# The attention stage of a two-stack float32 network on one core: dense tiles moved between attention units, and the stage's evictions rewritten

## Chip, core and metric

One core of a Trainium2 chip runs the whole program. The metric is the device time of one execution in microseconds (us).

## What is computed

256 tokens of width 1024, float32, pass through a first stack of four layers (each: half a SwiGLU block, a mixer, half a SwiGLU block) and a second stack of two layers. The change touches only the mixer of the second stack, so it is executed twice, once in each of its layers. Cut to that part, the reference is:

```
h = h + 0.5 * swiglu(rms_norm(h, g0), wi, wo)
n = rms_norm(h, g1)
aq, ak, av, bq, bkc, bvc, bks, bvs, bkw, bvw, bgate, cq, ck, cv, ga, gb, gc = split(n @ w_in)
ya = diff_attention(aq, ak, av)
yb = nsa_attention(bq, compress(bkc), compress(bvc), bks, bvs, bkw, bvw, sigmoid(bgate))
yc = swa_sink_attention(cq, ck, cv)
merged = sigmoid(ga)*(ya @ wb[0]) + sigmoid(gb)*(yb @ wb[1]) + sigmoid(gc)*(yc @ wb[2])
h = h + merged @ w_out
h = h + 0.5 * swiglu(rms_norm(h, g2), wi2, wo2)
```

Branch A has 4 heads with two score maps each and a norm of each head's output, branch B 8 heads with three kinds of keys each, branch C 8 heads.

## The kernel before

**Weights.** Every weight tile is 1 MB (128 x 2048 floats). SyncE loads it into one of RING = 3 `raw` buffers. ScalarE rounds it to `w_hi` (L513, in `split_hi`), VectorE subtracts to get `w_lo` (L891, in `split_lo`), and TensorE forms each product of three matmuls, hi*hi, lo*hi and hi*lo (L1584 to L1586, in `matmul3`). Tile n+3 may overwrite `w_hi`/`w_lo` of tile n only when TensorE has counted up `tile_used` for n. The helper that both engines call for this is `consumed(n)`, here ScalarE's (L515; VectorE's, L894, calls `split_lo`):

```
def consumed(n):
    act.wait_ge(tile_used, seen.next(tile_used))
    split_hi(n + RING)
```

Each engine runs its own instruction list in order, and the lists are written out by hand.

**PSUM.** Eight banks of 128 x 512 floats: `acc0..3` (attention scores and transposed probabilities, and the accumulators of the output projection) and `up0..3` (projections, attention outputs, gates).

**The stage (`mix`: ScalarE L740, VectorE L1362, TensorE L1940, GpSimd L2294)** has five parts.

1. A norm. `turn_norm` (L1646) keeps TensorE busy with dummy matmuls (L1644) until VectorE has 1/rms as a diagonal, and then transposes and scales x by matmuls against it (L1653). The norms before feed-forward blocks are of another kind (`norm_xs`): x is transposed unscaled by `turn_x` (L1665, matmuls at L1669), the first half of it inside the block before, and 1/rms is multiplied in when results leave PSUM. The tuple `XS` (L36) says which stages get that kind.
2. Projections: 19 weight tiles one after another. Nine are of 2 x 8 x 3 matmuls with 256 tokens moving (`up_matmuls`), three hold a key half of that kind and a value half of 128-column matmuls (`key_value`, L1951), four are the compression's hidden layer (`hidden`, L1962), two are for `AV` with 512 columns moving, and one has 24 columns (the gates of branch B).
3. Attention: 40 units (8 of A, 24 of B in the order sel, win, cmp, 8 of C) in steps i = 0 to 45. In step i TensorE forms the scores of unit i (L1742, L1743, or L2153 for cmp), transposes unit i-3 (L1749 to L1751, L2160) and multiplies values of unit i-4 (L2031 to L2033, L2055, L2056, L2052). VectorE reduces the scores (L1133), ScalarE takes exp (L657) and copies the transposed unit (L665), GpSimd scales (L2241).
4. Merge: per branch and half of the width, two gate tiles and one branch tile, 18 tiles in all, each in two pieces (`merge`, L2062) of 24 matmuls with 256 tokens moving. The table `PIECES` (L436) puts 16 pieces into steps 17 to 36, eight into steps 38 to 45 and the rest behind the loop. ScalarE in `merge` (L758) waits for `tile_used`, takes the sigmoid out of the bank and only then, in the next step, splits the next tile; VectorE (L1416) likewise multiplies by the gate first and keeps its split for two steps later.
5. Output projection: four tiles of 24 matmuls with 512 columns moving (`down_matmuls`), then the norm of the next feed-forward block, whose `turn_x` of both halves comes behind the last matmul.

Of the kernel before, what the change touches and what calls it, by code (L numbers as in the profile page):

```python
# [35 lines left out]
XS = ("ffn", "mla", "ple")  # L36
# [78 lines left out]
def build(nc, A, out, plan=None):  # L115
    plan = plan or full_plan()
    with ExitStack() as ctx:
# [7 lines left out]
        MIX_BANKS = 17  # L125

# [74 lines left out]
        BQ, CQ = carve(8448, 4, TOK), carve(11008, 4, TOK)  # L201
        KC = carve(9472, 2, TOK)
        BS, BW, CKV = carve(9984, 512), carve(10496, 512), carve(12032, 512)
        gB = carve(12544, NT, 24)
        KC2 = carve(12592, 2, 2, TOK)
        blk = carve(13616, 2, 16, 2 * NCMP)
        hid = arena[0:2 * NCMP, 14854:15366].rearrange("p (v n) -> p v n", v=2)
# [7 lines left out]
        merged = xn[:].rearrange("p t (m n) -> p (t m) n", n=TOK)  # L215
# [87 lines left out]
        gates_ready = sem("gates_ready")  # L303
        kc_ready = sem("kc_ready")
# [4 lines left out]
        hid_ready = sem("hid_ready")  # L309
        hid_turned = sem("hid_turned")  # L310
        hidT_ready = sem("hidT_ready")
        cmp_done = sem("cmp_done")
        cmp_ready = sem("cmp_ready")
        proj_ready = sem("proj_ready")
        ya_copied = sem("ya_copied")
        ya_ready = sem("ya_ready")
        merge_step = sem("merge_step")
        merge_gate = sem("merge_gate")
# [43 lines left out]
        def tiles_of(s):  # L362
# [39 lines left out]
            if s[0] == "mix":  # L402
                w, w1 = A["w_in_2"][s[1]], A["nsa_cmp_w1_2"][s[1]]
                wb, wo = A["w_branch_2"][s[1]], A["w_out_2"][s[1]]
                hidden = [up_tile(w1[v, 1024 * h:1024 * h + 1024, :], 0) for v in range(2) for h in range(2)]
                t = [up_tile(w, W_BC)] + [up_tile(w, W_AQ + CW * j) for j in range(4)]
                t += [cols_tile(w[512 * h:512 * h + 512, :], 4, W_AV, 512) for h in range(2)]
                t += [query_tile(w, W_BQ, j) for j in range(2)]
                t += [hidden[0], up_tile(w, W_BS), hidden[1], up_tile(w, W_BW), query_tile(w, W_CQ, 0)]
                t += [hidden[2], query_tile(w, W_CQ, 1), hidden[3], up_tile(w, W_CKV), cols_tile(w, KD, W_BG, 24)]  # L410
                for br in range(3):
                    for c in range(2):
                        t += [up_tile(w, W_G + D * br + 512 * c + CW * j) for j in range(2)]
                        t += [cols_tile(wb[br], 4, 512 * c, 512)]
                return t + [down_tile(wo, CW * j) for j in range(4)]
# [18 lines left out]
        YA_STEP = 16  # L434
        STEPS = NU + 6
        PIECES = {}  # L436
        for q in range(24):
            step_of = YA_STEP + 1 + int(1.3 * q) if q < 16 else NU - 2 + q - 16
            PIECES[step_of] = (q // 12, q // 6 % 2, q % 6)

        MIX_PROJ = 19
# [58 lines left out]
        def _(act):  # L500
# [239 lines left out]
            def mix(s, n0, bank0):  # L740
                for i in range(7):
                    consumed(n0 + i)
                for v in range(2):
                    act.wait_ge(blk_ready, seen.next(blk_ready))
                    nc.scalar.activation(blk_hi[:, v], blk[:, v], ACT.Copy).then_inc(blkhi_ready, 1)
                for i in range(7, MIX_PROJ):
                    consumed(n0 + i)
                    if i in (11, 16):

                        v = int(i == 16)  # L750
                        nc.scalar.activation(hid[:, v, :], acc[2 * v][0:2 * NCMP, 0:CW],
                                             ACT.Gelu_apprx_tanh).then_inc(hid_ready, 1)
                nc.scalar.activation(gB.rearrange("p t h -> p (t h)"), up[(bank0 + 14) % 4][:, 0:48],
                                     ACT.Sigmoid).then_inc(gates_ready, 1)

                late = []

                def merge(br, c, piece):  # L758

                    if piece % 2 == 0:  # L760
                        return
                    g = piece // 2
                    n = n0 + MIX_PROJ + 6 * br + 3 * c + g
                    act.wait_ge(tile_used, seen.next(tile_used))
                    if g < 2:
                        if g == 0 and (br or c):

                            act.wait_ge(merge_step, seen.next(merge_step))
                            if (br, c) == (2, 1):
                                parts_of_merged(0)  # L770
                        nc.scalar.activation((gate, prod)[g][:], up[g][:], ACT.Sigmoid).then_inc(merge_gate, 1)
                    late.append(n)

                def parts_of_merged(c):

                    for j in range(2 * c, 2 * c + 2):
                        if j >= 2:

                            consumed(n0 + MIX_PROJ + 18 + j - 2)
                        nc.scalar.activation(hT_hi[:, j % 2], merged[:, 2 * j:2 * j + 2, :],  # L780
                                             ACT.Copy).then_inc(mhi_ready, 1)

                for i in range(STEPS):
# [27 lines left out]
                    if i == YA_STEP:  # L811
                        parts_hi(4, 0, yT_hi, subln[:, s[1]:s[1] + 1], up)

                    while late:
                        split_hi(late.pop() + RING)
                    if i in PIECES:
                        merge(*PIECES[i])
                    if i >= NU:
                        while late:
                            split_hi(late.pop() + RING)  # L820
                for c in range(2):
                    for piece in range(6):
                        merge(2, c, piece)
                        while late:
                            split_hi(late.pop() + RING)
                act.wait_ge(merge_step, seen.next(merge_step))
                parts_of_merged(1)
                consumed(n0 + MIX_PROJ + 20)
                owed.append(n0 + MIX_PROJ + 21)
# [21 lines left out]
            for i, (s, n0) in enumerate(zip(plan, first)):  # L851
# [13 lines left out]
                elif s[0] == "tables":  # L865
                    tables(s[1])
                elif s[0] == "mix":
                    mix(s, n0, bank)
                    bank = (bank + MIX_BANKS) % 4
# [8 lines left out]
        def _(dve):  # L878
# [483 lines left out]
            def mix(s, n0, bank0):  # L1362
                n = n0
                bank = [bank0]

                def out(dst):

                    step(nc.vector.tensor_copy(dst, up[bank[0] % 4][:]))
                    bank[0] += 1
                    dve.sem_inc(bank_free, 1)  # L1370

                def flat(v):
                    return v.rearrange("p k n -> p (k n)")

                consumed(n)
                out(flat(KC))
                dve.sem_inc(kc_ready, 1)
                for j, dst in enumerate((AQ, AQ, AK, AK)):
                    consumed(n + 1 + j)
                    out(flat(dst[:, 2 * (j % 2):2 * (j % 2) + 2, :]))  # L1380
                consumed(n + 5)
                consumed(n + 6)
                for t in range(NT):
                    out(AV[:, t, :])

                dve.wait_ge(kc2_in, seen.next(kc2_in, 16 * 8))
                for v in range(2):
                    for j in range(16):
# [7 lines left out]
                places = [flat(BQ[:, 0:2, :]), flat(BQ[:, 2:4, :]), None, BS, None, BW, flat(CQ[:, 0:2, :]), None,  # L1396
                          flat(CQ[:, 2:4, :]), None, CKV]
                for i, place in enumerate(places):
                    consumed(n0 + 7 + i)
                    if place is not None:  # L1400
                        out(place)
                dve.wait_ge(hid_turned, seen.next(hid_turned))
                nc.vector.tensor_copy(hidT.rearrange("p v m n -> p (v m n)"), acc[1][:, 0:8 * NCMP]).then_inc(hidT_ready, 1)
                consumed(n0 + 18)
                dve.wait_ge(gates_ready, seen.next(gates_ready))
                bank[0] += 1
                dve.sem_inc(bank_free, 1)
                dve.wait_ge(cmp_done, seen.next(cmp_done))
                nc.vector.tensor_copy(kcT, up[bank[0] % 4][:, 0:2 * NCMP])
                step(nc.vector.tensor_copy(vc, up[(bank[0] + 1) % 4][0:NCMP, 0:128]))  # L1410
                dve.sem_inc(bank_free, 2)
                dve.sem_inc(proj_ready, 1)

                late, late_since = [], [0]

                def merge(br, c, piece):  # L1416
# [981 lines left out]
```

## Time and profile before

| | |
|---|---|
| median of 3 runs | 3616.49 us (3616.34 to 3617.01) |
| profiled execution | 3612.1 us, its span 3610.3 us |
| TensorE busy | 3432.8 us, 95% of the span |
| VectorE, ScalarE, GpSimd busy | 1848.2, 1561.2, 161.0 us |
| mean granted TensorE clock | 0.959 of full speed |
| share of the chain that ended last | TensorE 90%, VectorE 6%, ScalarE 3% |

The clock in the views is a share: 1.00 is 2.4 GHz, 0.50 is 1.2 GHz. In a timeline a line gives start, duration, engine, source line, operation, output and inputs, and in brackets the idle time before it with what ended it; the duration of a matmul contains its pipeline, so the pace of matmuls is read from the distance between starts.

### The profile page before, as it was taken

How to read it: one execution, taken by the hardware profiler on the slowest of the kernel's cores; microseconds unless marked ns; L12 is line 12 of the kernel's file. 1: busy time of each engine (PE TensorE's matmuls, PEld its weight loads, DVE VectorE, ACT ScalarE, POOL GpSimd, SP SyncE). 2: the span in 40 equal slices, each digit the busy share in tenths (PEclk: the TensorE clock that was granted, in tenths of full speed). 3: DMA queues.
4: the chain of work that ended last, by engine and by line, in shares of the span. 5: the costliest groups of instructions: out<-in, count | busy, mean ns of one | idle time of the engine just before them, and what ended most of it. 6: DMA issues, size and time to landing. Idle time of an engine off the chain costs nothing.

```text
span 3610.3 us, 42172 instructions
## 1 busy us (share of the span) xinstructions
PE 3432.8 (95%) x17691; PEld 2906.6 (81%) x17691; DVE 1848.2 (51%) x2378; ACT 1561.2 (43%) x1908; POOL 161.0 (4%) x253
## 2 busy tenths in 40 slices
PE   8999999859999999999999999999999999999998
PEld 6898888647888888787988788878887788878886
DVE  4455454564454564544554545524545545434545
ACT  4344444334444444443344343356444443454444
POOL 0000000020000000000000000033000000131000
PEclk9999999879999999999999999869999999789999
DMA  6545555414555445554555455503554555413553
GB/s 205 189 165 178 187 186 189 144 35 150 189 180 189 161 162 189 177 187 163 170 174 188 151 188 169 165 24 98 174 187 164 178 193 158 130 47 117 186 189 112
DMA packets 329835, 576.39 MB, mean 160 GB/s; under 512 B 45034, under 2 KB 148561, under 8 KB 329517
## 3 DMA queue, kind: packets, MB, share of 16 engines
q1 hardware_dynamic: 327116, 566.71, 47.2%
q0 software_dynamic: 2384, 6.63, 0.6%
q8 instruction: 139, 2.28, 0.3%
q10 hardware_dynamic: 144, 0.35, 0.0%
q14 instruction: 52, 0.42, 0.0%
HBM read 571.53 MB, written 1.08 MB: 159 GB/s over the span
## 4 chain that ended last, share of the span: by engine, by line
PE 90%; DVE 6%; ACT 3%; issue 1%; DMA 0%; POOL 0%; DVEq 0%; SPq 0%; ACTq 0%; POOLq 0%
PE up L1584 19%; PE up L1586 19%; PE up L1585 19%; PE acc L1584 7%; PE acc L1586 7%; PE acc L1585 7%; DVE w_lo L891 2%; ACT w_hi L513 2%; PE acc L1742 1%; PE up L1847 1%; PE up L2055 1%; PE acc L1749 1%; PE acc L1743 1%; PE acc L1653 0%; PE acc L1669 0%
## 5 line engine op out<-in xcount | busy, mean ns | idle before, releaser
L891 DVE TENSOR_TENSOR w_lo<-raw,w_hi 128x2048 fp32r<-128x2048 f32 x543 | 1244.2, 2292 | 1334.9 <-ACT w_hi L513 1329.8
L513 ACT ACTIVATE w_hi<-raw 128x2048 fp32r<-128x2048 f32 x543 | 1040.0, 1917 | 1507.5 <-PE up L1586 1127.8
L1584 PE MATMUL up<-w_hi,xT_hi 128*128 128x512 f32 (+2 forms) x2404 | 935.1, 389 | 49.8 <-DVE xT_lo L1003 28.0
L1586 PE MATMUL up<-w_hi,xT_lo 128*128 128x512 f32 (+2 forms) x2404 | 930.8, 387 | 0.0
L1585 PE MATMUL up<-w_lo,xT_hi 128*128 128x512 f32 (+2 forms) x2404 | 930.3, 387 | 0.0
L1584 PEld LDWEIGHTS up<-w_hi,xT_hi 128*128 128x128 f32 x2404 | 459.9, 191 | 143.7 <-issue 37.6
L1586 PEld LDWEIGHTS up<-w_hi,xT_lo 128*128 128x128 f32 x2404 | 460.0, 191 | 90.4
L1585 PEld LDWEIGHTS up<-w_lo,xT_hi 128*128 128x128 f32 x2404 | 460.4, 192 | 88.5
L1584 PE MATMUL acc<-w_hi,ff_hi 128*128 128x512 f32 (+1 forms) x1280 | 497.8, 389 | 3.5 <-DVE ff_lo L1022 3.5
L1586 PE MATMUL acc<-w_hi,ff_lo 128*128 128x512 f32 (+1 forms) x1280 | 491.8, 384 | 0.0
L1585 PE MATMUL acc<-w_lo,ff_hi 128*128 128x512 f32 (+1 forms) x1280 | 491.2, 384 | 0.0
L1584 PE MATMUL up<-xT_hi,w_hi 128*128 128x256 f32 x1168 | 339.3, 291 | 16.1 <-DVEq L1434 10.2
L1585 PE MATMUL up<-xT_lo,w_hi 128*128 128x256 f32 x1168 | 334.9, 287 | 0.0
L1586 PE MATMUL up<-xT_hi,w_lo 128*128 128x256 f32 x1168 | 334.8, 287 | 0.0
L1584 PEld LDWEIGHTS acc<-w_hi,ff_hi 128*128 128x128 f32 (+1 forms) x1280 | 235.3, 184 | 50.2 <-issue 4.7
L1586 PEld LDWEIGHTS acc<-w_hi,ff_lo 128*128 128x128 f32 (+1 forms) x1280 | 235.0, 184 | 49.0
L1585 PEld LDWEIGHTS acc<-w_lo,ff_hi 128*128 128x128 f32 (+1 forms) x1280 | 235.4, 184 | 45.7
L1584 PEld LDWEIGHTS up<-xT_hi,w_hi 128*128 128x128 f32 x1168 | 228.7, 196 | 25.5 <-issue 18.6
L1585 PEld LDWEIGHTS up<-xT_lo,w_hi 128*128 128x128 f32 x1168 | 228.8, 196 | 0.3
L1586 PEld LDWEIGHTS up<-xT_hi,w_lo 128*128 128x128 f32 x1168 | 228.6, 196 | 0.0
L2241 POOL TENSOR_SCALAR units<-units,rsum 128x256 f32<-128x256 f32 x80 | 67.0, 849 | 1057.6 <-DVE rsum L1143 1057.6
L657 ACT ACTIVATE units<-units,nmax 128x256 f32<-128x256 f32 (+1 forms) x192 | 80.4, 421 | 56.2 <-DVE nmax L1135 51.7
(276 smaller groups left out, 2500.2 us busy)
## 6 DMA issues: line engine op xcount, KB each, us to landing
raw<-in_ffn_down SPq DMA_DIRECT2D x88, 1024.0 KB, 4.8
raw<-in_ffn_gate SPq DMA_DIRECT2D x80, 1024.0 KB, 5.0
raw<-in_ffn_up SPq DMA_DIRECT2D x80, 1024.0 KB, 5.0
raw<-in_ffn_wi SPq DMA_DIRECT2D x80, 1024.0 KB, 5.0
raw<-in_ffn_wo SPq DMA_DIRECT2D x44, 1024.0 KB, 4.8
raw<-in_w_in SPq DMA_DIRECT2D x44, 1024.0 KB, 5.1
raw<-in_conv_w_in SPq DMA_DIRECT2D x24, 1024.0 KB, 5.0
raw<-in_w_branch SPq DMA_DIRECT2D x12, 1024.0 KB, 4.9
```

What stands on the lines that cost most here:

```text
L513: nc.scalar.activation(w_hi[n % RING][:], raw[n % RING][:], ACT.Copy).then_inc(hi_ready, 1)
L657: last = nc.scalar.activation(S[b][:, lo:hi], S[b][:, lo:hi], ACT.Exp, bias=nmax[b][:, i:i + 1], scale=-1.0, accum_out=esum[b][:, i:i + 1])
L891: nc.vector.tensor_tensor(w_lo[n % RING][:], raw[n % RING][:], w_hi[n % RING][:].bitcast(F32), ALU.subtract).then_inc(lo_ready, 1)
L1584: pe.matmul(ps, lh, rh, start=start, stop=False)
L1585: pe.matmul(ps, lh, rl, start=False, stop=False)
L1586: return pe.matmul(ps, ll, rh, start=False, stop=stop)
L1742: pe.matmul(ps[:, 0:256], q[:, P:TOK], k, start=True, stop=True)
L1743: pe.matmul(ps[:, 256:384], q[:, 0:P], k[:, 0:P], start=True, stop=True).then_inc(scores_done, 1)
L1749: pe.transpose(ps[:, 0:P], S[b][:, 256:384], ident)
L1847: last = pe.transpose(dst[:, at:at + P], ff_prod[:, t, m * P:(m + 1) * P], ident)
L2055: pe.matmul(o, kv[:, cols], PT[u % 2][:, 0:TOK], start=starts, stop=False)
L2241: last = pool.tensor_scalar(S[b][:, lo:hi], S[b][:, lo:hi], rsum[b][:, t:t + 1], factors[t], ALU.mult, ALU.mult if factors[t] is not None ...
```

## The change

- `XS` now has "mix": the stage gets the norm of the feed-forward blocks, with `turn_x(0)` inside the block before and `turn_x(1)` inside the first pair of tiles. 1/rms is broadcast to all partitions by one matmul of a ones matrix against the diagonal (`rb`), and is multiplied in when banks are evicted, by `rb` where tokens are columns, by `rstd` where tokens are rows.
- The projections are regrouped: three value halves and the 24 gate columns form one pair of tiles with 408 columns moving (`v`), the keys `kk` one tile, `ck` half a tile. Their number stays 19, that of all tiles 41.
- The gates and the branch products are computed with tokens as rows: `g0..g5` are pairs of tiles (4 parts of 12 matmuls, 512 columns moving), `b0..b5` one tile (2 parts of 12). `merged` is held by tokens and transposed at the end, by 16 transposes.
- Only `av`, `bc`, `aq0`, `aq1`, `ak0`, `ak1` come ahead of the attention loop. All else is cut into parts that follow the units: two parts a step in steps 0 to 6, one a step from step 7 on, and the last five behind the loop. The banks `up0` and `up1` take all of them, `up2` and `up3` the attention outputs. A group waits until the group that held its bank is evicted.
- The output projection ends by token halves, with the next stage's `turn_x(0)` ahead of the last 12 matmuls.

```diff
-XS = ("ffn", "mla", "ple")
+XS = ("ffn", "mla", "mix", "ple")
...
+        YA_STEP = 18
+        KINDS = {"ws": 2, "k": 1, "hid": 2, "pair": 4, "b": 2, "": 1}
+        GROUPS = [("av", "pair", (2, 3), 0, 1), ("bc", "ws", (0,), 0, 1)]
+        GROUPS += [(name, "ws", (b,), 0, 1) for name, b in (("aq0", 1), ("aq1", 0), ("ak0", 1), ("ak1", 0), ("q0", 1),
+                                                            ("q1", 0), ("kk", 1))]
+        GROUPS += [("hid0", "hid", (0,), 1, 0), ("hid1", "hid", (1,), 1, 0), ("v", "pair", (0, 1), 1, 1),
+                   ("hidT", "", (0,), 0, 1), ("cmp", "", (1,), 0, 1), ("q2", "ws", (0,), 0, 1), ("q3", "ws", (1,), 0, 1),
+                   ("ck", "k", (0,), 0, 1), ("g0", "pair", (0, 1), 1, 0), ("ya", "", (0, 1), 0, 2),
+                   ("g1", "pair", (0, 1), 1, 0), ("g2", "pair", (0, 1), 1, 0), ("b0", "b", (0, 1), 0, 1),
+                   ("b1", "b", (0, 1), 0, 1)]
+        GROUPS += [(f"g{j}", "pair", (0, 1), 1, 0) for j in (3, 4, 5)]
+        GROUPS += [(f"b{j}", "b", (0, 1), 0, 1) for j in (2, 3, 4, 5)]
...
+            BEFORE[name] = [holder[b] for b in in_banks if b in holder]
...
+        for j, piece in enumerate(parts_in("q0", "q1", "kk", "hid0", "hid1", "v")):
+            PIECES.setdefault(j // 2, []).append(piece)
+        for j, piece in enumerate(parts_in("hidT", "cmp", "q2", "q3", "ck", "g0", "ya", "g1", "g2", "b0", "b1", "g3", "g4",
+                                           "g5", "b2", "b3", "b4", "b5")):
+            PIECES.setdefault(min(7 + j, STEPS), []).append(piece)
+        BLOCKS_AT = {1: 0, 2: 1}
...
@@ ScalarE @@
+                def dense(name, part):
+                    done = tile_end(name, part)
+                    if done is not None:
+                        consumed(n0 + done)
+                    if part + 1 < KINDS[KIND[name]]:
+                        return
...
+                    elif name[0] == "g":
+                        for t in range(NT):
+                            last = nc.scalar.activation(gates_of[int(name[1])][:, t, :], up[t][:], ACT.Sigmoid,
+                                                        scale=rstd[:, t:t + 1])
+                        last.then_inc(dense_act, 1)
...
@@ VectorE @@
+                def dense(name, part):
+                    done = tile_end(name, part)
+                    if done is not None:
+                        consumed(n0 + done)
+                    if part + 1 < KINDS[KIND[name]]:
+                        return
+                    if name in places:
+                        scaled(places[name], name)
...
+                    elif name[0] == "b":
+                        merge(int(name[1]))
+                def merge(j):
+                    br, c = divmod(j, 2)
+                    dve.wait_ge(dense_act, ACT_IN * s[1] + EVICTED[f"g{j}"][0])
+                    cols = slice(FW * c, FW * c + FW)
+                    for t in range(NT):
+                        dst = merged[:, t, cols] if br == 0 else gates_of[j][:, t, :]
+                        last = nc.vector.tensor_tensor(dst, gates_of[j][:, t, :], up[t][:], ALU.mult)
+                    last.then_inc(dense_dve, 1)
+                    if br == 0:
+                        return
+                    dve.wait_ge(dense_dve, DVE_IN * s[1] + EVICTED[f"b{j}"][1])
+                    for t in range(NT):
+                        last = nc.vector.tensor_tensor(merged[:, t, cols], merged[:, t, cols], gates_of[j][:, t, :], ALU.add)
+                    if br == 1:
+                        step(last)
+                    else:
+                        last.then_inc(merged_ready, 1)
...
@@ TensorE @@
+                def dense(name, part):
+                    kind, b = KIND[name], BANKS[name][0]
+                    n = n0 + TILE_AT[name]
+                    if part == 0:
+                        for held in BEFORE[name]:
+                            evicted(held)
+                    if part == 0 and kind or kind == "hid" or (kind == "pair" and part == 2):
+                        pe.wait_ge(lo_ready, seen.next(lo_ready))
...
                 for i in range(STEPS):
...
+                    for piece in PIECES.get(i, ()):
+                        dense(*piece)
...
+                for c in range(2):
+                    pe.wait_ge(merged_ready, seen.next(merged_ready))
+                    for k in range(4):
+                        for t in range(NT):
+                            at = (k % 2) * TOK + t * P
+                            last = pe.transpose(up[2 * (1 - c) + k // 2][:, at:at + P],
+                                                merged[:, t, FW * c + P * k:FW * c + P * k + P], ident)
...
+                down_half(*downs[2], 0, False)
...
+                down_half(*downs[3], 0, True)
+                down_half(*downs[2], 1, False).then_inc(tile_used, 1)
+                residuals[0] += 1
+                turn_x(0)
+                down_half(*downs[3], 1, True)
```

## Rows read from the trace of the kernel before

**Rows 1.** The page's head: span, and busy time of TensorE

```profile
span 3610.3 us, 42172 instructions
PE 3432.8 (95%) x17691; PEld 2906.6 (81%) x17691; DVE 1848.2 (51%) x2378; ACT 1561.2 (43%) x1908; POOL 161.0 (4%) x253
```

**Rows 2.** Windows: length, busy PE, PEld, DVE, ACT, POOL (count), clock, DMA, GB/s

```profile
2212.90:2224.50 11.60, 9.41 (x70) 9.22 (x68) 6.83 (x19) 5.45 (x11) 0.00 (x0) 0.85 0.56 182
2224.50:2341.50 117.00, 111.52 (x862) 107.98 (x861) 62.36 (x73) 42.26 (x30) 4.16 (x8) 0.93 0.61 168
2341.50:2399.80 58.30, 56.07 (x192) 41.55 (x192) 17.53 (x114) 26.46 (x107) 20.38 (x38) 0.50 0.06 19
2399.80:2500.00 100.20, 100.20 (x660) 83.18 (x659) 38.79 (x135) 65.55 (x152) 32.89 (x50) 0.98 0.24 76
2212.90:2588.90 376.00, 358.48 (x2337) 316.70 (x2336) 172.43 (x384) 176.13 (x336) 60.95 (x97) 0.89 0.39 120
3003.80:3376.00 372.20, 354.70 (x2338) 313.62 (x2336) 172.52 (x384) 176.24 (x336) 60.91 (x97) 0.89 0.40 121
```

**Rows 3.** Timeline of TensorE, steps of attention with and without a dense piece

```profile
2443.36 0.69 PE L1742 MATMUL acc<-arena 64*128 64x256 f32 x2
2445.47 0.39 PE L1584 MATMUL up<-xT_hi,w_hi 128*128 128x256 f32 x1
2448.54 0.61 PE L2153 MATMUL acc<-arena 64*128 64x15 f32 x4
2450.20 0.39 PE L1584 MATMUL up<-xT_hi,w_hi 128*128 128x256 f32 x1
...
2453.27 0.70 PE L1742 MATMUL acc<-arena 64*128 64x256 f32 x2
...
2455.16 0.70 PE L1742 MATMUL acc<-arena 64*128 64x256 f32 x2
```

**Rows 4.** Timeline of TensorE, x transposed ahead of a feed-forward block's last matmuls

```profile
2773.27 1.03 PE L1669 MATMUL acc<-consts,x 128*128 128x128 f32 x8
2774.06 0.48 PE L1584 MATMUL acc<-w_hi,ff_hi 128*128 128x512 f32 x1
2774.84 0.39 PE L1584 MATMUL acc<-w_hi,ff_hi 128*128 128x512 f32 x1
...
2776.20 0.39 PE L1584 MATMUL acc<-w_hi,ff_hi 128*128 128x512 f32 x1
```

**Rows 5.** Timeline of ScalarE and VectorE after a tile's last matmul

```profile
2242.03 1.91 ACT L513 ACTIVATE w_hi<-raw 128x2048 fp32r<-128x2048 f32 x1 [3.85 <-PE up L1586]
...
2244.05 2.29 DVE L891 TENSOR_TENSOR w_lo<-raw,w_hi 128x2048 fp32r<-128x2048 f32 x1 [2.87 <-ACT w_hi L513]
...
2246.26 0.68 DVE L1368 COPY arena<-up 128x512 f32<-128x512 f32 x1
...
2443.46 0.60 ACT L771 ACTIVATE gate<-up 128x512 f32<-128x512 f32 x1 [0.52 <-PE up L1586]
```

**Rows 6.** Timeline of ScalarE, two sigmoids of another stage behind a table load

```profile
2792.69 1.28 ACT L842 ACT_TABLE_LOAD   x1
2793.98 1.26 ACT L842 ACTIVATE gate<-up,rstd 128x512 f32<-128x512 f32 x2
```

**Rows 7.** Timeline of TensorE, the first matmul behind four waits

```profile
2281.66 0.58 PE L1584 MATMUL up<-xT_hi,w_hi 128*128 128x256 f32 x1 [2.98 <-DVE w_lo L891]
...
2502.97 0.36 PE L1584 MATMUL up<-xT_hi,w_hi 128*128 128x256 f32 x1 [1.98 <-DVEq L1434]
...
2528.66 0.36 PE L1584 MATMUL up<-xT_hi,w_hi 128*128 128x256 f32 x1 [3.10 <-DVEq L1434]
...
2588.92 0.77 PE L1584 MATMUL up<-w_hi,xT_hi 128*128 128x512 f32 x1 [2.31 <-DVE xT_lo L1003]
```

**Rows 8.** Windows behind the second and third of these waits, columns as in rows 2

```profile
2503.00:2506.40 3.40, 3.40 (x18) 3.40 (x19) 2.94 (x4) 0.00 (x0) 3.04 (x2) 0.56 0.02 5
2528.70:2532.10 3.40, 3.40 (x29) 3.40 (x30) 2.20 (x1) 0.00 (x0) 0.00 (x0) 1.00 0.20 44
```

More of the change, by code:

```diff
@@ new lines, in build, with tile_end, parts_in @@
+        MIX_DOWN, ACT_IN, DVE_IN = at, n_act, n_dve
+        def tile_end(name, part):
+            kind = KIND[name]
+            if kind == "ws" or kind == "b":
+                return TILE_AT[name] if part == 1 else None
+            if kind == "pair":
+                return TILE_AT[name] + part // 2 if part % 2 else None
+            return TILE_AT[name] + part if kind else None
+        def parts_in(*names):
+            return [(name, part) for name in names for part in range(KINDS[KIND[name]])]
@@ L738, in tables, with mix @@
                 nc.scalar.activation(ssh[:, 4:8], ssh[:, 0:4], ACT.Exp).then_inc(tab_act, 1)
-            def mix(s, n0, bank0):
-                for i in range(7):
+            def mix(s, n0):
+                act.wait_ge(rs_ready, seen.next(rs_ready))
+                for i in range(TILE_AT["q0"]):
                     consumed(n0 + i)
[L743 to L760, printed above, removed]
-                        return
[L762 to L781, printed above, removed]
@@ L867, in _ @@
                 elif s[0] == "mix":
[L868 to L869 removed]
+                    mix(s, n0)
                 elif s[0] == "ple":
@@ L1360, in flipped_tables, with broadcast_rstd @@
                     dve.wait_ge(tab_dve, seen.next(tab_dve))
[L1362 to L1382, printed above, removed]
-                for t in range(NT):
-                    out(AV[:, t, :])
-                dve.wait_ge(kc2_in, seen.next(kc2_in, 16 * 8))
-                for v in range(2):
+            def broadcast_rstd():
+                for t in range(NT):
+                    last = nc.vector.tensor_scalar(diag[:, t, :], ident, rstd[:, t:t + 1], None, ALU.mult)
+                last.then_inc(diag_ready, 1)
@@ L1395, in mix @@
                                             ALU.subtract).then_inc(blklo_ready, 1)
[L1396 to L1414, printed above, removed]
@@ L1438, in parts_of_merged @@
[L1438 to L1444 removed]
+                places = {"q0": BQ[:, 0:2, :], "q1": BQ[:, 2:4, :], "kk": BK, "q2": CQ[:, 0:2, :], "q3": CQ[:, 2:4, :]}
@@ L2005, in mix, with evicted @@
-                for g in range(2):
-                    for m in range(2):
-                        last = pe.matmul(vb[0:NCMP, 64 * g:64 * g + 64], hidT[:, 1, m, NCMP * g:NCMP * g + NCMP],
-                                         w2[:, s[1], 1, m, :], start=m == 0, stop=m == 1)
-                last.then_inc(cmp_done, 1)
-                pe.wait_ge(proj_ready, seen.next(proj_ready))
+                def evicted(name):
+                    a, d = EVICTED[name]
+                    if a:
+                        pe.wait_ge(dense_act, ACT_IN * s[1] + a)
+                    if d:
+                        pe.wait_ge(dense_dve, DVE_IN * s[1] + d)
@@ L2037, in values_bc @@
                 def values_bc(u, br, kind, h, ends):
+                    if br == 1 and h == 0 and kind == "sel":
+                        evicted("v")
+                        pe.wait_ge(ya_copied, seen.next(ya_copied))
                     pe.wait_ge(pt_ready, seen.next(pt_ready))
-                    if br == 1 and h == 0 and kind == "sel":
-                        pe.wait_ge(ya_copied, seen.next(ya_copied))
                     starts = kind == "sel" or br == 2
@@ L2103, in mix @@
-                drain_banks()
+                drain_banks()
+                first_pair(n0, FW, [up[2][:], up[3][:]])
+                pe.wait_ge(diag_ready, seen.next(diag_ready))
+                pe.matmul(acc[0][:, 0:TOK], ones[:], diag[:].rearrange("p t n -> p (t n)"), start=True,
+                          stop=True).then_inc(rb_done, 1)
+                for piece in parts_in("bc", "aq0", "aq1", "ak0", "ak1"):
+                    dense(*piece)
+                pe.wait_ge(rb_done, seen.next(rb_done))
@@ L2104, in mix @@
+                evicted("av")
                 for i in range(STEPS):
@@ L2133, in mix @@
-                    if i in PIECES:
-                        merge(*PIECES[i])
+                    for piece in PIECES.get(i, ()):
+                        dense(*piece)
                 pe.wait_ge(nmax_ready, seen.next(nmax_ready, 2))
+                for piece in PIECES[STEPS]:
+                    dense(*piece)
+                pe.wait_ge(olo_ready, seen.next(olo_ready, 2))
                 for c in range(2):
-                    for piece in range(6):
-                        merge(2, c, piece)
```

472 lines of the change are left out of this document (245 added, 227 removed).

## Prediction

> **What bounds the kernel now.** The page's head comes first: TensorE is busy for 95% of the span [rows 1], so the time is what TensorE has to issue, at the clock it is granted, plus its waits. The windows come next. From the last matmul of the block before to the first of the block after, the stage takes 376.0 us in one layer and 372.2 us in the other [rows 2], mean 374.1. The reader is to see three things there. The norm takes 11.6 us. The 58.3 us of the first 17 attention steps run at clock 0.50 throughout, with TensorE busy nearly all the time: the same matmuls at 1.00 would take about half. The 100.2 us in which attention is mixed with dense pieces run at 0.98. The timeline then gives prices at full clock. A step of attention costs 2.11 us (2443.36 to 2445.47), 1.66 where a cmp unit leads (2448.54 to 2450.20) and 1.89 where a sel unit leads (2453.27 to 2455.16) [rows 3]. A piece of 24 matmuls of 256 columns costs 3.07 us [rows 3]. A tile of 48 such matmuls has a period of 3.85 + 1.91 = 5.76 us [rows 5], 0.12 a matmul, so entering a piece costs 0.19. With 512 columns six matmuls take 1.36 us (2774.84 to 2776.20) [rows 4], 0.227 each, where two of 256 take 0.240.
>
> **TensorE's work after the change**, for one stage, at full clock.
> - Ahead of the loop: `av` 48 x 0.227 = 10.9, `turn_x(1)` 0.8 [rows 4], the 1/rms broadcast and its wait 1.0 (estimate), five tiles 28.8. Sum 41.5.
> - Steps 0 to 6: attention 10.0 (the pipeline fills), three tiles 17.3, four hidden tiles 96 x 0.12 = 11.5, `v` 48 matmuls of 408 columns at 0.18 (between 0.12 and 0.227) 8.8, entries 1.3. Sum 48.9.
> - Steps 7 to 42: 24 B units 8 x (1.89 + 2.11 + 1.66) = 45.3, 8 C units 16.9, one A unit 2.0, three emptying steps 3.8, `q2`, `q3`, `ck` 14.4, six gate pairs 6 x 48 x 0.227 = 65.4, `b0`, `b1` 10.9, small transposes and compression 2.3, 36 entries 6.8. Sum 167.8.
> - The rest: `b2..b5` 21.8, last values 0.8, 16 + 16 transposes 3.2, output projection 96 x 0.227 = 21.8. Sum 47.6.
>
> Total 305.8. The stage of before stands against it with 374.1 + 1.6, since the block behind it starts at half clock (its matmul of 512 columns lasts 0.77 instead of 0.39 [rows 4, 7]). The work saved is thus 70 us a stage: some 29 of half-clock attention, 10 of norm, 12 to 16 of waits, 8 of a 24-column tile whose 48 matmuls go at half clock, and the rest regrouping, less the entries.
>
> **The waits that it adds.** All dense groups share `up0` and `up1`. A gate pair takes both, and the next group starts only when both are evicted. What delays the eviction is the order within `dense`: ScalarE and VectorE first call `consumed`, which splits the tile three ahead, and evict afterwards. Behind the last matmul of a gate pair: start 0.10 (2443.36 to 2443.46) [rows 3, 5], split 1.91 [rows 5], table load 1.28, two sigmoids 1.26 [rows 6], hand-over 0.1: 4.65 us. TensorE has only the next attention step to fill it. Four such ends leave 2.5 us, one (before a sel step) 2.8, the one before `b2` (attention over, 0.8 to do) 3.85: 16.7. Behind a branch tile VectorE's chain counts: 0.10 + 1.91 + 0.11 + 2.29 + two products at 0.68 [rows 5] = 5.8. `b0` leaves 3.9, `b1` 4.1; `b2`, `b3`, `b4` have nothing beside them and leave 5.8 each: 25.4. After `b5` come the products and two additions, 7.2, beside 0.8 of transposes: 6.4. Smaller ones: `ck` to `g0` 2.9, `v` to `hidT` 3.5 (sigmoid of 24 columns, then VectorE's split and two scalings), `hid1` to `v` 2.0, a hidden tile late because VectorE builds the compression blocks ahead of its splits 4.0 (the same work leaves 2.98 now [rows 7]), the next block's first tile 1.9. Sum 62.8 in 17 waits. The ends: a wait is no negative time, and if the chains overlap more than I see, about 45; if VectorE, whose next score reduction stands behind the split, falls further back, 75.
>
> Queued behind these: ScalarE's exp of the next unit and VectorE's scores are late by up to 5 us, but TensorE needs them two to four steps later, at over 4.8 us a step. SyncE loads tile n+3 when `w_lo` of n is ready, as before, and 41 tiles in over 300 us press nothing. GpSimd's copies of KC start earlier and are needed in step 1. These I cost at nothing.
>
> The table load is 1.28 us in this trace [rows 6]. The Trainium skill (ScalarE: Activation LUTs, Table sets: the hidden batching unit) says otherwise: batch activations by set, since each change of set costs about 2.7 us. By it seven loads a stage would be 1.4 longer each, 10 us a stage, and the time about 3664. The measured row decides.
>
> **The clock.** After waits of 2.98, 1.98 and 2.31 us the matmuls behind them run at half speed: a 256-column matmul of 0.58 instead of 0.36, a window at clock 0.56, a 512-column one of 0.77 [rows 7, 8]. After 3.10 us nothing of the kind happened (1.00) [rows 8]. A half-speed stretch costs some 1.5 to 1.7 us where TensorE has work. Four waits thus cost 1.6 + 1.5 + 0 + 1.6, 1.2 on average; 17 waits 20 us. The ends are 0 and 17 x 1.7 = 29; 1.2 is the mean of the only rows.
>
> **Sum.** 306 + 63 + 20 = 389 against 375.7: 13.6 us longer, 27 for two stages. The profiled execution took 3612.1 us and would take 3639; it stands 4.4 below the median of 3616.5, against which the forecast is **3644 us**.
>
> **The rivals.**
> - *Waits as above, clock held.* The pieces between waits are dense, and the mixed stretch of now keeps 0.98 [rows 2]. Against it: three of four exposed waits lowered the clock [rows 7, 8], one of only 1.98 us. 306 + 63 = 369, 7 us less a stage: 3603. Chance 0.25.
> - *The waits are mostly covered* (the other side). Its place is the chain behind a group's last matmul. If the eviction went ahead of the split, a gate pair would free its banks after about 1.5 to 2.7 us and a branch tile after 1.5, nearly covered by a step of 1.66 to 2.11. Then some 15 of waits and 4 of clock remain: 325, 51 less a stage, 3515. It decides once waits and clock together stay under 70 a stage. Now `merge` evicts first, and rows 2 show no wait in the mixed stretch. The diff's order speaks against it. Chance 0.17, the values between it and the first rival included.
> - *Every wait halves the clock.* 17 x 1.7 = 29: 398, 22 above the stage of before, 3661. For it: longer waits than the 2 to 3 us of rows 7 are the rule at the stage's end. Chance 0.15. The Trainium skill (TensorE: Matmul & The Clock Gate, A second HAM failure mode: psum-queue depth-cycling) states this mechanism: short idle stretches between groups of matmuls, as their banks cycle, make the clock swing and cost throughput.
> - *Half clock keeps itself up*, as in the 58.3 us of rows 2. At half speed the work of steps 7 to 42 takes 336 instead of 168, less some 30 of waits and the 20 for single dips: 118 above the forecast a stage, 3880. The dense pieces lifted the clock within one piece before. Chance 0.05.
>
> **How the numbers follow.** The forecast has the remaining 0.38, for 3610 to 3680 around it (waits 45 to 75, clock 0 to 29 at the ends: 3557 to 3685). A measurement of this kernel can tell about 0.2%, 7 us. Faster: the second rival and two thirds of the first, 0.34. Within 0.2%: the rest of the first and the low edge of the forecast, 0.13. Slower: 0.53. The range 3560 to 3690 leaves out most of the second rival and the last, under 0.2. The likeliest case's own range is 3610 to 3680.
>
> **What would show it.** Right: TensorE's waits before first matmuls of `g`, `b` groups on "ACT gates" and on VectorE's products, 2.5 and 4 us in the loop and near 6 us behind it, five or six of them; ScalarE's table load and sigmoids directly behind a split; clock dips spread over the stage; attention steps of 2.1 instead of 3.4 us; no wait where the norm was; busy TensorE time of the stage down by some 50 us, with the stage no shorter. Wrong: no such waits (then the second rival), or waits without dips (the first); also a stage whose busy time has not fallen, which would mean that attention stayed at half clock.

## The result, and the profile after

The changed kernel takes 3668.5 us (median of 4 runs, 3668.2 to 3674.2) against 3616.4 us of the kernel before, measured beside it: ratio 1.015 (95% interval 1.013 to 1.017), 52 us slower. The forecast was 3644, the range 3560 to 3690. Sign and order of size were right. The 24 us by which it lay too low have one main cause, the clock.

The page's head of the changed kernel, against [rows 1]; of part 2, the granted clock in 40 slices; of part 4, the chain by engine:

```profile
span 3666.4 us, 39845 instructions
PE 3394.4 (93%) x16471; PEld 2815.1 (77%) x16471; DVE 1846.1 (50%) x2387; ACT 1568.5 (43%) x1918; POOL 143.1 (4%) x253
...
PEclk9999999889999999998999999888999999898999
...
PE 85%; DVE 7%; ACT 6%; issue 2%; DMA 1%; SPq 0%; DVEq 0%; ACTq 0%
```

TensorE has 1220 instructions fewer and is busy for 38 us less, and yet the span is 56 us longer: what it won went into idle time, and part of its busy time went at a lower clock.

The windows of the two mixing stages, from the stage's first matmul to the next block's first, columns as in [rows 2]; the third is the start of a branch tile, the fourth a stretch that begins half a us behind a wait of 3.83 us:

```profile
2212.00:2614.30 402.30, 338.06 (x1720) 269.44 (x1718) 170.09 (x382) 179.08 (x336) 52.02 (x97) 0.89 0.37 109
3030.30:3433.50 403.20, 337.61 (x1720) 269.66 (x1718) 169.95 (x383) 179.08 (x336) 51.96 (x97) 0.89 0.37 109
2572.00:2575.40 3.40, 3.40 (x8) 2.72 (x9) 1.22 (x2) 0.00 (x0) 0.00 (x0) 0.50 0.84 297
2532.50:2535.80 3.30, 3.30 (x9) 2.60 (x8) 0.09 (x1) 0.00 (x0) 0.00 (x0) 0.50 0.86 295
```

Before, a stage took 376.0 and 372.2 us [rows 2]; now 402.3 and 403.2. The sum of the differences, 57, makes up the difference of the spans (3666.4 less 3610.3 = 56). Of a stage 338 us are busy and 64 to 66 idle. The mean clock is 0.89 as before, but for another reason: then it was mainly one stretch at 0.50, now it is 15 short ones, spread over all the stage. The long stretch lasted 75 us, more than the 58 us that [rows 2] show of it; in the kernel before:

```profile
2329.40:2404.40 75.00, 70.27 (x267) 55.38 (x267) 22.70 (x117) 31.20 (x112) 20.60 (x38) 0.50 0.09 29
```

TensorE's waits in the first stage (line, tile, what it waited for: us in total, times, longest):

```profile
PE up L1627 <- DVE arena L1481: 17.0, 3, 5.7
PE up L1627 <- ACT arena L813: 10.5, 4, 2.7
PE up L1627 <- DVE xn L1481: 7.7, 2, 4.0
PE up L2163 <- DVE xn L1487: 6.0, 1, 6.0
PE up L1627 <- ACT arena L799: 4.2, 1, 4.2
PE up L1627 <- DVE arena L1409: 4.1, 2, 3.8
PE up L1627 <- ACT gate L813: 3.8, 1, 3.8
PE up L2039 <- issue: 3.5, 1, 3.5
PE up L1627 <- DVE w_lo L922: 3.0, 2, 2.8
PE up L2062 <- ACT arena L813: 2.5, 1, 2.5
PE up L1627 <- DVE xT_lo L1034: 1.9, 1, 1.9
```

Sum 64.2 us (65.2 in the second stage, where the wait on L799, the gelu of a hidden tile, is 5.7). L813 is the gates' sigmoid, L1481 and L1487 the products and additions of `merge`, L1409 the scaling of `ck`.

The same waits one by one in the timeline of TensorE, with the duration of the first matmul behind them. A 512-column one lasts 0.39 at full clock [rows 4], 0.47 behind a gap, and 0.77 at half clock. A first matmul of 0.47 does not yet show that the clock held: behind the one at 2531.96 it fell half a us later (the fourth window above).

```profile
2379.03 1.94 PE L2062 MATMUL up<-consts,arena 128*128 128x128 f32 x8 [2.50 <-ACT arena L813]
2406.93 0.77 PE L1627 MATMUL up<-w_hi,xT_hi 128*128 128x512 f32 x1 [2.73 <-ACT arena L813]
2431.90 0.47 PE L1627 MATMUL up<-w_hi,ff_hi 128*128 128x512 f32 x1 [2.51 <-ACT arena L813]
2445.16 0.76 PE L1627 MATMUL up<-w_hi,ff_hi 128*128 128x512 f32 x1 [3.75 <-DVE xn L1481]
...
2531.96 0.47 PE L1627 MATMUL up<-w_hi,ff_hi 128*128 128x512 f32 x1 [3.83 <-ACT gate L813]
2544.88 0.77 PE L1627 MATMUL up<-w_hi,ff_hi 128*128 128x512 f32 x1 [5.64 <-DVE arena L1481]
2558.43 0.76 PE L1627 MATMUL up<-w_hi,ff_hi 128*128 128x512 f32 x1 [5.67 <-DVE arena L1481]
2572.00 0.76 PE L1627 MATMUL up<-w_hi,ff_hi 128*128 128x512 f32 x1 [5.67 <-DVE arena L1481]
2586.92 1.97 PE L2163 MATMUL up<-consts,xn 128*128 128x128 f32 x8 [6.05 <-DVE xn L1487]
```

The chain that makes a wait behind a gate pair, in the timeline of ScalarE; its parts are those of [rows 5, 6]:

```profile
2402.34 1.91 ACT L558 ACTIVATE w_hi<-raw 128x2048 fp32r<-128x2048 f32 x1 [2.80 <-PE up L1629]
2404.27 1.28 ACT L813 ACT_TABLE_LOAD   x1
2405.56 1.26 ACT L813 ACTIVATE arena<-up,rstd 128x512 f32<-128x512 f32 x2
```

And the one behind a branch tile, ScalarE's split and then VectorE:

```profile
2566.37 1.91 ACT L558 ACTIVATE w_hi<-raw 128x2048 fp32r<-128x2048 f32 x1 [11.65 <-PE up L1629]
2568.41 2.29 DVE L922 TENSOR_TENSOR w_lo<-raw,w_hi 128x2048 fp32r<-128x2048 f32 x1 [8.74 <-ACT w_hi L558]
2570.62 1.28 DVE L1481 TENSOR_TENSOR arena<-arena,up 128x512 f32<-128x512 f32 x2
```

1.91, 2.29 and 1.28 (two products) with the hand-overs are 5.67 us, the wait at 2572.00.

### The profile page after: what moved, and what is told of

It reads as the page before. It is cut to its first block, busy times and chain, and to the rows that moved or that the text cites. A ratio compares the mean times of both kernels' runs of the same rounds, so it can differ in the third digit from the quotient of the medians.

```text
span 3666.4 us, 39845 instructions
## 1 busy us (share of the span) xinstructions
PE 3394.4 (93%) x16471; PEld 2815.1 (77%) x16471; DVE 1846.1 (50%) x2387; ACT 1568.5 (43%) x1918; POOL 143.1 (4%) x253
## 3 DMA queue, kind: packets, MB, share of 16 engines
HBM read 571.53 MB, written 1.08 MB: 156 GB/s over the span
## 4 chain that ended last, share of the span: by engine, by line
PE 85%; DVE 7%; ACT 6%; issue 2%; DMA 1%; SPq 0%; DVEq 0%; ACTq 0%
PE up L1627 19%; PE up L1628 18%; PE up L1629 18%; PE acc L1627 7%; PE acc L1629 7%; PE acc L1628 7%; ACT w_hi L558 3%; DVE w_lo L922 3%; PE up L1902 1%; PE acc L1797 1%; PE up L2118 1%; DVE xT_lo L1034 1%; PE acc L1724 0%; ACT L813 0%; ACT xT_hi L623 0%
## 5 line engine op out<-in xcount | busy, mean ns | idle before, releaser
L1627 PE MATMUL up<-w_hi,xT_hi 128*128 128x512 f32 (+1 forms) x2500 | 999.6, 400 | 90.7 <-DVE xT_lo L1034 27.2
L1628 PE MATMUL up<-w_lo,xT_hi 128*128 128x512 f32 (+1 forms) x2500 | 987.1, 395 | 0.0
L1629 PE MATMUL up<-w_hi,xT_lo 128*128 128x512 f32 (+1 forms) x2500 | 986.4, 395 | 0.0
L1627 PE MATMUL acc<-w_hi,ff_hi 128*128 128x512 f32 x1216 | 481.6, 396 | 3.5 <-DVE ff_lo L1053 3.5
L1629 PE MATMUL acc<-w_hi,ff_lo 128*128 128x512 f32 x1216 | 474.5, 390 | 0.0
L1628 PE MATMUL acc<-w_lo,ff_hi 128*128 128x512 f32 x1216 | 473.9, 390 | 0.0
L1627 PEld LDWEIGHTS acc<-w_hi,ff_hi 128*128 128x128 f32 x1216 | 229.0, 188 | 49.5 <-issue 4.7
L1629 PEld LDWEIGHTS acc<-w_hi,ff_lo 128*128 128x128 f32 x1216 | 228.6, 188 | 48.8
L1628 PEld LDWEIGHTS acc<-w_lo,ff_hi 128*128 128x128 f32 x1216 | 229.2, 188 | 45.1
L1627 PE MATMUL up<-xT_hi,w_hi 128*128 128x256 f32 x784 | 224.9, 287 | 0.0
```

The lines of the kernel that those rows point to most:

```text
L1627: pe.matmul(ps, lh, rh, start=start, stop=False)
L1628: pe.matmul(ps, lh, rl, start=False, stop=False)
L1629: return pe.matmul(ps, ll, rh, start=False, stop=stop)
```

## The experiments

Theory A: TensorE's waits come from the order split, then evict, and each costs clock besides. B: the splits are the limit, whichever comes first. C: the clock falls for other reasons than the waits. D: the table load is off the path.

**Evict first** (`e1_both`; `e2_act` is ScalarE's half alone, `e3_dve` VectorE's):

```
 def dense(name, part):
     done = tile_end(name, part)
     if done is not None:
-        consumed(n0 + done)              # wait tile_used, split
-    if part + 1 < KINDS[KIND[name]]:
-        return
-    <evict>
+        wait tile_used
+    if part + 1 == KINDS[KIND[name]]:
+        evict(name)
+    if done is not None:
+        split_hi(n0 + done + RING)       # VectorE: split_lo
```

> ScalarE and VectorE evict a tile's last bank first and split the incoming weight tile after it. Theory A (a wait of TensorE is split plus eviction, one after the other, and each wait of some us costs about 2 us of half clock besides: 20 us of clock foreseen a stage, 36 found): ScalarE's split of 1.9 us leaves some 7 waits and VectorE's of 2.3 us some 7 others, so about 29 us of wait a stage go, and where a wait falls below 1 us its clock loss goes too, another 12 to 20: 3668 falls to 3560 to 3590. Rival B (the split was on the path whichever comes first): the splits come later by the eviction, waits on the low half of a weight tile appear instead, and the time stays within 3640 to 3668. Rival C (the half clock has nothing to do with the waits): only the 29 us of wait go, 3610, with as many half-clock stretches as before.

> Only ScalarE evicts first. Theory A: the waits behind gate pairs fall from 2.5 to about 0.7 us, the one before the first branch tile of the second run of them from 3.8 to 1.9, the one after the hidden tiles from 4.2 to 2.3; those before branch tiles (5.7) stay. About 13 us of wait and 8 to 12 of clock a stage: 3620. Rival B: 3668 within 10 us, with new waits on the split. Rival C: 3642.

> Only VectorE evicts first. Theory A: the four waits of 5.7 us before and behind the last branch tiles fall to 3.4, the two of 3.8 to 4.0 of the first ones and the one behind the key tile to 1.6; the waits behind gate pairs stay. About 16 us of wait and 3 to 8 of clock a stage: 3625. Rival B: 3668 within 10 us. Rival C: 3636. If the waits of the two engines are independent, e2's gain and e3's add to e1's.

Measured: both 3541.9 us (ratio to before 0.980, 0.978 to 0.981), ScalarE alone 3631.6 (1.004, 1.003 to 1.006), VectorE alone 3592.0 (0.993, 0.992 to 0.995). Against the changed kernel that is 127, 37 and 76 us less. The timeline of TensorE in the run of both:

```profile
2374.32 0.77 PE L1637 MATMUL up<-w_hi,xT_hi 128*128 128x512 f32 x1 [4.65 <-DVE ff_lo L1477]
2491.26 0.47 PE L1637 MATMUL up<-w_hi,ff_hi 128*128 128x512 f32 x1 [0.61 <-ACT gate L818]
2498.37 0.47 PE L1637 MATMUL up<-w_hi,ff_hi 128*128 128x512 f32 x1 [1.43 <-DVE arena L1491]
2505.57 0.47 PE L1637 MATMUL up<-w_hi,ff_hi 128*128 128x512 f32 x1 [1.48 <-DVE arena L1491]
2512.71 0.47 PE L1637 MATMUL up<-w_hi,ff_hi 128*128 128x512 f32 x1 [1.43 <-DVE arena L1491]
2521.14 1.09 PE L2173 MATMUL up<-consts,xn 128*128 128x128 f32 x8 [1.83 <-DVE xn L1497]
```

None of the three met its expectation: the run of both lies 18 us under its range, ScalarE's 12 us over 3620, VectorE's 33 us under 3625. The waits of 5.7 fell to 1.4, not to 3.4 as expected: VectorE's half of the split starts only when ScalarE's is done, so evicting first takes both (1.91 + 2.29) out of the chain. The 33 us by which the VectorE run beat its expectation fit this, though their parts were not measured. B falls: no wait on `w_lo` took the place, those left are of 1.2 us at most. Behind the waits of 1.4 us the clock held. Behind the last row's wait of 1.83 us, which another of 1.80 follows, it did not (windows of the same run, columns as in [rows 2]):

```profile
2498.40:2512.80 14.40, 11.49 (x49) 8.91 (x50) 9.81 (x11) 3.88 (x3) 0.00 (x0) 1.00 0.46 166
2522.30:2529.00 6.70, 4.96 (x12) 3.93 (x13) 3.38 (x5) 0.62 (x2) 0.00 (x0) 0.50 0.49 157
```

ScalarE's run gave less than expected, because the wait behind `v` grew (3.5 to 6.0) and a new one of 4.7 us came up behind `ya`, which the wait before it had hidden (in the run of both it is the first row of the timeline).

In the view of waits from 2200 us on, TensorE's sum was 141 us in the changed kernel, 119, 88 and 57 in these three. So 22, 53 and 84 us of wait went, and 37, 76 and 127 us of time: half as much again.

**Filling a wait** (`e4_fill` with 40, `e5_fill24` with 24). No wait is shortened; TensorE is only kept at work in the last three of a stage.

```
+    # before ("b4", 0), ("b5", 0) and the second half of the merge
+    for _ in range(24):
+        pe.matmul(acc[0][:, 0:P], ident, ident, start=True, stop=True)
```

> Forty useless 128-column matmuls (4.7 us at full clock) fill each of the last three waits of a stage (before the last two branch tiles and before the second half of the merge is turned). The sum of work and wait is left as it was. Theory A: TensorE keeps its full clock across them, what stands behind them runs at 0.227 us a matmul from the first on, and the half-clock stretches of these three waits go: about 6 us a stage, 3668 to 3656. Rival C (the clock falls for other reasons): 3668 or a little more, the stretches stay. If the fill is longer than the wait at the clock it gets, up to 2 us a wait are lost: 3680.

> The fill again, with 24 matmuls for each of the last three waits of a stage: at the 0.224 us that each took in the run with forty (9 us in place of the wait of 5.7) they take 5.4 us and end about with the wait. Theory A: each wait stays 5.7 us long, the clock stays at full speed behind it, and the 24 matmuls behind it take 5.5 us, where they took 7.9: 2.4 us less for each of the six, so 3668 to 3654. Rival C (the clock falls whether TensorE rests or not): 3668.

Measured: 3678.7 and 3655.3 us (1.018, 1.016 to 1.019; 1.013, 1.010 to 1.016). The timeline of the first:

```profile
2558.69 9.09 PE L2158 MATMUL acc<-consts 128*128 128x128 f32 x80
2567.54 0.48 PE L1627 MATMUL up<-w_hi,ff_hi 128*128 128x512 f32 x1
2567.85 0.40 PE L1628 MATMUL up<-w_lo,ff_hi 128*128 128x512 f32 x1
```

and of the second, whose first matmul behind each fill is shown:

```profile
2552.84 5.52 PE L2158 MATMUL acc<-consts 128*128 128x128 f32 x48
...
2558.66 0.47 PE L1627 MATMUL up<-w_hi,ff_hi 128*128 128x512 f32 x1 [0.31 <-DVE arena L1481]
2558.97 0.39 PE L1628 MATMUL up<-w_lo,ff_hi 128*128 128x512 f32 x1
...
2570.04 0.47 PE L1627 MATMUL up<-w_hi,ff_hi 128*128 128x512 f32 x1 [0.31 <-DVE arena L1481]
```

The 40 took 9.1 us, since each of these matmuls stands in the trace as two, at 0.11 us each (0.227 for both). That was my mistake in sizing: 9.1 against a wait of 5.7 is more than the clock gives back. With 24 the fill is 5.5 us, as long as the wait was. From one branch tile's start to the next's it is now 11.4 us (2558.66 to 2570.04), where the changed kernel has 13.6 (2558.43 to 2572.00), with the same wait in it. The granted clock is 1.00 behind each fill. 2.2 us of a period is thus clock alone, and C falls. Six filled waits gave 13 us.

**Bank by bank** (`e6_banks` on top of evict first; `e7_banks_split_first` without it). The parts of a gate pair go in the order token half 0 of both tiles, then token half 1; each bank has its own count and is evicted while the other is filled.

```
-    h, t = divmod(part, 2)
+    t, h = divmod(part, 2)
...
-    for t in range(NT):
-        last = activation(gates[:, t, :], up[t][:], Sigmoid, scale=rstd[:, t:t + 1])
-    last.then_inc(dense_act, 1)
+    activation(gates[:, t, :], up[t][:], Sigmoid, scale=rstd[:, t:t + 1]).then_inc(dense_act, 1)
```

> On top of evicting first (3542): gate pairs and branch tiles are worked and evicted bank by bank (all of token half 0, then all of token half 1), so that one bank is emptied while the other is filled. Theory A: the waits behind gate pairs and branch tiles (1.4 to 1.5 us each, four a stage, and the 0.6 and 1.2 ones) go, the last one before the merge is turned falls from 1.8 to about 1.2; those behind the hidden tiles, the key tile and the block parts stay. About 8 to 10 us a stage and half a dozen us of clock at most: 3515 to 3528. Rival B (these short waits are lost only in name, since the split is the next limit): 3542 within 8 us, with waits on the low half of the weight tiles.

> Bank by bank as before, but with the changed kernel's own order in ScalarE and VectorE (split first, then evict). Theory A: ScalarE's 2.5 us for a gate pair's last bank fits beside the next bank's 5.4 us of matmuls, so the waits behind gate pairs go; VectorE's 4.9 us for a branch tile's last bank stand against 2.7 us of matmuls, so about 2.2 us stay in place of 5.7; the waits behind the key tile (3.8) and the hidden tiles stay. About 30 us of wait and 15 to 20 of clock a stage less than 3668: 3565 to 3580. If bank order and evict-first were each enough by itself, it would come to 3542 or less.

Measured: 3533.9 us (0.979, 0.976 to 0.983) and 3561.6 (0.987, 0.984 to 0.989). The second lies 3 us below its range; its waits before branch tiles are 2.3 to 2.4 us, as foreseen. In the first only 8 us were gained, where 14 to 27 were expected. The waits of 1.4 us went, but in the loop others came up (on `w_lo` 2.1 us, on copied probabilities 1.1 to 2.9), and as the short waits had cost no clock, nothing came on top.

**No table loads for the gates** (`e8_tanh` on the changed kernel, `e9_banks_tanh` on bank by bank):

```
-    activation(gates, up, Sigmoid, scale=rstd)
+    activation(gates, up, Tanh, scale=rstd / 2)
...
-    tensor_tensor(dst, gates, up, mult)
+    scalar_tensor_tensor(dst, gates, 1.0, up, add, mult)   # the half: scale=0.5 where merged is copied
```

> The changed kernel in its own order, with the six gates as a tanh of half the argument (the factor one half goes into the merged tile's copies), which is meant to spare ScalarE the two table loads of 1.28 us of each gate pair. Theory A (the load of 1.28 us lies in the chain of split, load and two evictions): the five waits behind gate pairs fall from 2.5 to 2.7 us to about 1.3, the one before the first branch tile behind them from 3.8 to 2.6; where 1.3 us are left no clock is lost, since waits of 1.4 to 1.9 us lost none in the run that evicts first. 8 us of wait and 8 to 12 us of clock a stage: 3628 to 3638. Rival D (the load runs ahead of the wait, beside the split): nothing, 3668.

> The same on top of bank by bank with eviction first (3534). Theory A: only what is left of ScalarE's waits there (1.0 us before the turn of the first branch, 1 to 2 us on copied probabilities) can go: 2 to 4 us a stage, 3526 to 3531. Rival D: 3534.

Measured: 3646.4 us (1.009, 1.007 to 1.011) and 3524.7 (0.975, 0.974 to 0.977). The timeline of TensorE in the first:

```profile
2386.09 0.49 PE L1628 MATMUL up<-w_hi,xT_hi 128*128 128x512 f32 x1 [2.38 <-DVE ff_lo L1468]
2408.43 0.47 PE L1628 MATMUL up<-w_hi,xT_hi 128*128 128x512 f32 x1 [1.31 <-ACT arena L813]
2429.20 0.47 PE L1628 MATMUL up<-w_hi,ff_hi 128*128 128x512 f32 x1 [1.08 <-ACT arena L813]
...
2522.43 0.47 PE L1628 MATMUL up<-w_hi,ff_hi 128*128 128x512 f32 x1 [2.40 <-ACT gate L813]
```

The waits of 2.73 and 2.51 are 1.31 and 1.08: 1.42, the load of 1.28 and 0.14 more. D falls. The clock behind these two is full; behind a later one of 1.31 us (it ends at 2480.99) it was at 0.50 from 2482.0 to 2485.4, and behind the 0.47 of the last row from 2523.0 to 2526.3. The whole gave 22 us and not 30 to 40: behind `ya` a new wait of 2.4 came up, and this execution reached the stage 4 us later in code that no edit touched (its first wait ends at 2220.16, at 2215.96 in the changed kernel). These 4 us come with the clock as well: between 740 and 820 us, in the first stack, this execution has 10.2 us more at half speed than the changed kernel's. From the first wait to the next block it is 384.7 against 398.3 us, 27 us for two stages, an estimate from the first. The run on top of bank by bank gave 9 us, 1 below its range.

**The last wait of the loop** (`e10_ya_first`, on top of the ninth run): the split of `g0`'s last tile is done only after `ya`'s eviction, on both engines.

```
-    if done is not None:
+    if done is not None and (name, part) != ("g0", 3):
         split_hi(n0 + done + RING)
+    if name == "ya":
+        split_hi(n0 + tile_end("g0", 3) + RING)
```

> On top of that, the split of the first gate pair's last weight tile waits until the turned first branch is evicted. Theory A: TensorE's wait of 4.4 us behind that turn falls to about 2, and the clock with it is kept: 3 to 5 us a stage, 3518 to 3524. Rival B (the split is the next limit, 4 us late): a new wait of 2 to 3 us on that tile's low half, no gain against the run before.

Measured: **3516.0 us** (0.973, 0.971 to 0.975), the best of all, 100 us below the kernel before and 152 below the changed one, with all of the computation in it, and 2 us below its range: the wait behind `ya`, 4.25 us in the run before, went altogether, where 2 us were expected to stay. The stage's window there, columns as in [rows 2], from the end of the stage's first wait to the next block's first matmul:

```profile
2220.22:2539.41 319.19, 306.89 (x1698) 247.31 (x1699) 167.37 (x378) 163.05 (x323) 52.30 (x97) 0.98 0.45 134
```

and in the changed kernel:

```profile
2215.96:2614.28 398.32, 334.25 (x1698) 266.42 (x1699) 166.20 (x377) 176.33 (x332) 52.02 (x97) 0.89 0.37 108
```

The same 1698 instructions of TensorE are busy for 306.9 us at clock 0.98 and for 334.3 at 0.89. The difference in length is 79 us: 27 of busy time and 52 of waits.

## Why the prediction was right, and where it was off

- **TensorE's work: 306 us foreseen, about 305 found.** A stage is busy for 338 us. In the clock's records of the first one, 15 stretches at half speed hold 70.5 us of that. At full clock they would be 33 shorter, so 305. That is an estimate from the best run: there the same 1698 instructions hold 12.3 us of half clock, 58.1 less than the 70.5, and are busy for 27.4 us less, 0.47 for each us. The pace says the same: 0.427 us from one 512-column matmul to the next at half clock (nine from 2572.56 to 2576.40), 0.227 at full [rows 4], so a matmul at half clock loses 0.47 of its time, not one half.
- **Waits: 62.8 us in 17 foreseen, 64.2 and 65.2 found.** Behind gate pairs 2.5, 2.5, 2.7, 2.7 and 2.5 (with the last ahead of the turn of `ya`), then 3.8 before `b2`; behind branch tiles 3.75, 3.98, 5.64, 5.67, 5.67, then 6.05. The terms were 2.5 to 2.8, 3.85, 3.9, 4.1, 5.8 and 6.4. Three were missed, and cancel in part: `hid1` to `v` was 4.2 and 5.7 instead of 2.0, because gelu too loads a table and stands behind a split (this entry was given no chain of its own), `ck` to `g0` was 3.8 instead of 2.9, and the late hidden tile cost 2.8 instead of 4.0.
- **Clock: 20 us foreseen, about 35 found (33, and 1.6 more of half clock at the start of the next block, behind its wait of 1.9). This is the step that failed.** The step took 1.2 us for each of 17 waits, the mean of four cases of which one had lost nothing [rows 7, 8], and capped it at 1.7. It measured 2.0 on average. Both parts of it were too low. One wait in four was to leave the clock whole; of the 17 in the first stage one did, that of 2.51 us which ends at 2431.90, and behind the 16 others a stretch at half speed is on record. And a dip was priced as those of [rows 7, 8], whose stretches hold 3.4 us of TensorE's work at most; of the 15 here six hold 2.9 to 3.4, the other nine 3.6 to 9.8. Behind a wait of 5.7 us, 24 matmuls took 7.9 us (2572.00 to 2579.90) instead of 5.5, so 2.4. None of the four rows stood behind a wait of over 3.1 us. The upper end, 29, was too low by 6.
- **Sum.** 305 + 64.7 + 34.7 = 404, against 389 foreseen and 375.7 before: 28.6 a stage, 57 for both, where 27 was foreseen. Of the medians it is 52, since the profiled execution of before stood 4 us below its median.
- **The rivals.** "Waits as above, clock held" (3603) fell with the granted clock in the stage (0.89) and with the fill. "Every wait halves the clock" (3661) came nearest. Nearly every wait did halve it, but this rival priced each at 1.7. The Trainium skill's statement beside it (TensorE: Matmul & The Clock Gate, A second HAM failure mode: psum-queue depth-cycling) agrees with this trace: short idle stretches between groups of matmuls, here 17 in 400 us, cost 35 us of throughput. "The waits are mostly covered" is what the kernel is with evict first: 3515 foreseen, 3542 measured, since 23 us of waits stayed a stage, not 15. "Half clock keeps itself up" did not happen: the mean is 0.89.
- **The table load** is 1.28 us in each of the 12 loads at L813, and taking them out moved the waits by 1.42. The Trainium skill's 2.7 us for a change of set (ScalarE: Activation LUTs, Table sets: the hidden batching unit) is not borne out: from the end of ScalarE's split to the first sigmoid it is 1.31 us (2404.25 to 2405.56), nearly all of it the load. That its use made the forecast 3664, nearer to the result, is chance: the missing microseconds were the clock's.
- Of the signs announced, one came out otherwise: the stage's busy time fell by 20 and 17 us (358.5 and 354.7 in [rows 2]), not by some 50, since half-clock matmuls count as busy. The prediction's own sum, 306 of work and 20 of clock, would have made it some 30.
- **What the change did bring** is hidden in it: 70 us of TensorE's work a stage were foreseen as saved, 375.7 less 306, and 375.7 less 305 is 71. The waits and their clock gave back 99, most of it through the order of two calls.

What stays open: why of waits of the same length, 2.51 us for one, some were followed by half clock and some not, and why the clock in the first stack, which no edit touched, differs by some us from one kernel to another.

## What to carry to other kernels

When two groups of matmuls share their PSUM banks, the chain from the last matmul to a free bank is a price paid once for each group: put the eviction ahead of everything else on its engine, work the banks one after the other, and look for what stands in front (a split, a table load, a late helper). Price a wait of TensorE of several us at its length and half as much again for the clock behind it, and don't take that surcharge from waits that are shorter than those to come. After a wait is removed, read the waits again: the next one (here `ya`'s, 4.7 us) has been standing behind it.

## What the runs showed of the hardware

- The longer TensorE's wait, the more often the granted clock was at half during it or within 1.5 us behind it. In the two stages of the twelve kernels it was so for all 101 waits of 3.5 to 6.1 us, for 77 of 96 of 2.0 to 3.5 us, for 22 of 32 of 1.7 to 2.0 us, and for 8 of 47 of 0.9 to 1.7 us. A wait of 5.7 us whose time was filled with matmuls without use left it whole.
- A us of TensorE's work at half clock cost 0.47 us, not one half (27.4 us for 58.1).
- Per microsecond of wait taken away, the time fell by 1.4 to 1.7 us (84 and 127, 53 and 76, 22 and 37; in the best run 104 and 152). Where tanh shortened waits of 2.5 to 2.7 us to 1.1 to 1.3, it was 2.3 (12 and 27, the 4 us ahead of the stage left out).
- A plain f32 matmul of 128 columns on a 128x128 tile stands in the trace as two instructions and takes 0.23 us at full clock (24 of them 5.52 us).
- A tanh beside exp needed no table load: with it, the loads at the gates' line went from 12 to none, and those at exp's line from 19 to 9 (in the changed kernel's own order).
